# Page numbers of a paged cache: read once into SyncE registers instead of before each page load

## The reference

```
past = lambda pool: pool[layer, page_table].reshape((B, -1) + pool.shape[3:]).astype(z.dtype)
k_all = jnp.concatenate([past(cache_k), k], axis=1)
v_all = jnp.concatenate([past(cache_v), v], axis=1)
```

## Time and profile before

| | us |
|---|---|
| median of 3 runs | 941.52 |
| the three runs | 938.66, 941.52, 942.02 |
| the profiled execution, its own time | 942.91 |
| its span in the trace | 941.0 |
| TensorE busy (matmul) | 859.9 (91%) |
| VectorE, ScalarE, GpSimd busy | 448.6, 334.4, 89.4 |
| mean granted TensorE clock, of full speed | 0.961 |
| moved by DMA | 105.82 MB, mean 112 GB/s |

### The profile page before, as it was taken

One profiled execution on the slowest core, in us unless ns is written; L12 is line 12 of the kernel. 1 busy time (PEld: TensorE's weight loads), 2 busy tenths in 40 slices (PEclk: granted clock), 3 DMA queues, 4 the chain that ended last, 5 costly groups with the idle time before them and its releaser, 6 DMA issues.

```text
span 941.0 us, 11347 instructions
## 1 busy us (share of the span) xinstructions
PE 859.9 (91%) x4136; PEld 645.4 (69%) x4136; DVE 448.6 (48%) x862; ACT 334.4 (36%) x627; POOL 89.4 (10%) x136
## 2 busy tenths in 40 slices
PE   2799999999988986879978999999999999999997
PEld 0377556687735554435767788888888888888875
DVE  0251656999766873231365432234233433344256
ACT  2452543233445562220366342233212341133232
POOL 2141200112523330001010000000000000000000
PEclk9989999998978897999998999999999999999999
DMA  9733311123276566757201222221232222321202
GB/s 312 278 99 100 99 45 45 28 74 101 91 241 224 180 215 202 234 155 235 87 9 56 76 89 90 90 69 65 91 90 75 62 89 90 89 71 64 90 1 100
DMA packets 68778, 105.82 MB, mean 112 GB/s; under 512 B 6987, under 2 KB 32215, under 8 KB 68715
## 3 DMA queue, kind: packets, MB, share of 16 engines
q1 hardware_dynamic: 64194, 96.48, 32.1%
q0 software_dynamic: 3296, 6.39, 2.2%
q10 hardware_dynamic: 1232, 2.23, 0.7%
HBM read 100.04 MB, written 5.15 MB: 112 GB/s over the span
## 4 chain that ended last, share of the span: by engine, by line
PE 75%; DVE 7%; ACT 3%; issue 2%; DMA 2%; SPq 1%; POOL 0%; DVEq 0%; ACTq 0%
PE bank L742 71%; PE bank L745 3%; DMA raw<-in_ada_w 1%; DVE score L1775 1%; DVE small L1771 1%; DVE probs L1851 1%; ACT stage L1261 1%; DVE keys L1656 1%; ACT w_split L1236 1%; SPq L542 1%; SPq L560 0%; DVE x_res L1952 0%; DVE act_lo L1656 0%; DMA pages<-in_cache_k 0%; ACT pv_rows L1261 0%
## 5 line engine op out<-in xcount | busy, mean ns | idle before, releaser
L742 PE MATMUL bank<-act_hi,w_split 128*128 128x512 f32 (+1 forms) x800 | 265.5, 399 | 1.5 <-DVE q_lo L1659 1.5
L742 PEld LDWEIGHTS bank<-act_hi,w_split 128*128 128x128 f32 (+1 forms) x800 | 150.9, 189 | 37.9 <-issue 3.9
L493 DVE TENSOR_TENSOR w_split<-raw,w_split 128x2048 fp32r<-128x2048 f32 (+2 forms) x47 | 105.5, 2247 | 124.6 <-ACT w_split L1236 124.5
L742 PE MATMUL bank<-w_split,hid_hi 128*128 128x512 f32 x512 | 159.2, 392 | 0.0
L742 PE MATMUL bank<-act_lo,w_split 128*128 128x512 f32 (+1 forms) x400 | 157.1, 393 | 0.0
L1236 ACT ACTIVATE w_split<-raw 128x2048 fp32r<-128x2048 f32 (+2 forms) x48 | 89.3, 1863 | 92.3 <-PE bank L742 92.3
L742 PEld LDWEIGHTS bank<-w_split,hid_hi 128*128 128x128 f32 x512 | 95.9, 188 | 20.7
L742 PE MATMUL bank<-w_split,hid_lo 128*128 128x512 f32 x256 | 100.2, 391 | 0.0
L742 PEld LDWEIGHTS bank<-act_lo,w_split 128*128 128x128 f32 (+1 forms) x400 | 75.5, 189 | 14.5
L1261 ACT ACTIVATE stage<-bank 128x512 f32<-128x512 f32 (+3 forms) x51 | 30.1, 590 | 100.3 <-PE bank L742 92.1
L742 PE MATMUL bank<-w_split,act_s 128*128 128x512 f32 (+1 forms) x248 | 60.7, 387 | 1.5 <-DVE out_t L1958 1.5
(11 more groups left out here) (249 smaller groups left out, 1094.8 us busy)
## 6 DMA issues: line engine op xcount, KB each, us to landing
raw<-in_w_ff SPq DMA_DIRECT2D x32, 1024.0 KB, 5.3
raw<-in_ada_w SPq DMA_DIRECT2D x20, 1024.0 KB, 5.6
raw<-in_w_in SPq DMA_DIRECT2D x10, 1024.0 KB, 5.2
pages<-in_cache_k SPq DMA_DIRECT2D x32, 256.0 KB, 3.1
v_pages<-in_cache_v SPq DMA_DIRECT2D x32, 256.0 KB, 3.0
pages<-in_ada_w SPq DMA_DIRECT2D x4, 1024.0 KB, 13.0
raw<-in_w_out SPq DMA_DIRECT2D x4, 1024.0 KB, 6.4
x_in<-in_x_prompt SPq DMA_DIRECT2D x1, 2048.0 KB, 14.8
```

The costliest lines, as they stand in the source:

```text
L493: return ops.tensor_tensor(lo, r, hi.bitcast(F32), ALU.subtract)
L742: return nc.tensor.matmul(out, lhsT, rhs, start=start, stop=stop, skip_group_check=True)
```

## The change

The reads leave `load_pages`. SP waits once for the table, behind the wait of the piece `k` 0, and after each piece from `k` 0 on reads four page numbers into registers of its own, until it has all 32; they are kept to the end of the pages. Key and value page loads take the address from the kept register.

```diff
@@ -536,11 +536,6 @@
-            def page_of(i):
-                if i == 0:
-                    sp.wait_ge(S["table_in"], 16)
-                return sp.value_load(table[0:1, i:i + 1], min_val=0, max_val=ck.shape[0] - 1)
-
@@ -551,14 +546,18 @@
             for n in range(2, AT[("k", 0)]):
                 load_piece(n)
 
+            page = []
+            sp.wait_ge(S["table_in"], 16)
             for n in range(AT[("k", 0)], AT[("ada", 12)] + 2):
                 load_piece(n)
+                for i in range(len(page), min(len(page) + 4, DB * NPG)):
+                    page.append(sp.value_load(table[0:1, i:i + 1], min_val=0, max_val=ck.shape[0] - 1))
 
             def load_pages(b, cache, slots, landed):
 
                 for g in range(NPG):
                     sp.dma_start(slots[:, b % 2, g, :],
-                                 cache[bass.ds(page_of(b * NPG + g), 1)].rearrange("o p n -> (o p) n"))\
+                                 cache[bass.ds(page[b * NPG + g], 1)].rearrange("o p n -> (o p) n"))\
                         .then_inc(landed[b % 2], 16)
```

## The result

| | before | changed |
|---|---|---|
| median of 12 runs each, us | 943.24 | 939.06 |
| the runs | 938.66 to 946.84 | 932.47 to 943.42 |
| profiled execution, us | 942.91 | 936.69 |
| its span, us | 941.0 | 934.8 |
| mean granted TensorE clock | 0.961 | 0.968 |

The account below looks back on a forecast made before the run. TensorE was taken to bound the kernel, waiting in the decode attention for pages SP issued late. Savings of 4.7 + 3.0 + 0.3 + 0.6 = 8.6 us from median 941.5 gave 932.9, stated as 933.2 us; range 930 to 938.

Parts of the forecast that it names:

- the clock falls all the same: Rival: short idle times in the decode attention still halve TensorE's clock, so 5.6 us saved, 935.9 us; chance 0.22.
- Part 1: First decode pair: pages issued without reads cut TensorE's wait for sequence 2's keys from 5.43 to 0.7 us, saving 4.7.
- under 5.5: Sign that the forecast is right: SP issues the twelve pages of the first burst within 5.5 us of about 347.
- The row of 370 GB/s: Rate taken for the first burst from modulation weight loads: eleven pages in 7.8 us, landing at 358.2.
- Part 2: Behind the wait for sequence 2's keys TensorE's clock no longer falls to half: 3.0 us saved.
- Part 3: Last decode pair: its 0.28 us wait for value pages goes, 0.3 us saved; the half clock there stays.
- Part 4: Start of the prompt's attention: earlier first key pages let the next modulation weight load land sooner, 0.6 us saved.
- Part 5: Page number reads moved between the eight weight loads are covered by SP's free time there: cost 0.
- The premise that a gain before 500 us comes through whole: From 500 us on TensorE is busy 431.66 of 435 us, so whatever is gained earlier is kept in full.
- the transfers did not bind at 247 GB/s: Rival: page transfers, not their issue, limit the first burst, so 1.8 us saved, 939.7 us; chance 0.11.
- crowding did not choke the queue: Rival: twelve pages in flight slow each other, under 160 GB/s for a loss over 0.5%, 947.0 us; chance 0.03.
- the change did what it says: Denies the rival that register copies cost as much as the reads, burst 8.8 us, time 941.5; chance 0.04.

Follow-up runs that it names:

- e5: The kernel before, with six matmuls whose result nothing reads put in TensorE's wait for the key pages of sequence 2; ratio 0.9975 to the kernel before.
- e1: The changed kernel with kept page numbers only for the twelve pages of the first burst, other pages reading theirs at the load; 0.9956 of the kernel before.
- e2: The changed kernel, all 32 numbers kept, but the twelve pages of the first burst read theirs again at the load; 0.9997 of the kernel before.
- e3: The kernel before with each page number of the first burst read twice, the first value thrown away; ratio 1.0087 to the kernel before.
- e4: The changed kernel with the keys of sequences 2 and 3 issued before the values of 0 and 1; 0.9925 of the kernel before.
- e8: The changed kernel, but the first eight key pages (sequences 0 and 1) read their numbers at the load; 0.9944 of the kernel before.
- e7: The changed kernel with matmuls that nothing reads in TensorE's waits for the softmax of each pair; 0.9904 of the kernel before.
- e9: The changed kernel with keys of sequences 2 and 3 first, first eight key pages read at load, unread matmuls in the softmax waits; 0.9888 of the kernel before.

## Why the prediction was right, and where not

The saving was forecast as 8.6 us and measured as 5.3, between 3.0 and 7.5, so it was overrated. The direction holds, and on the footing of the three runs 936.2 lies in the range, whose top was 938. The median of 939.06 itself is above it, because the kernel before was 1.7 us slower in the larger sample too. The time alone would speak for the rival that the clock falls all the same, with 5.6 us saved; only the trace of pair 1 and e5 tell that the forecast's mechanism was at work, and that the time came out near that rival for another reason, a fall two pairs later.

- **Part 1, the wait: 4.7 forecast, 4.05 measured.** The last page went out at 352.7 and the transfers took over, as said. The twelve issues took 6.15 us and not under 5.5: a value page without its address arithmetic went out every 0.48 us and not every 0.44, and one issue took 0.78. The row of 370 GB/s was a little too good: the burst moved 350 by its window, and the eleven pages behind the first landed at about 340 (between 350.0 and 358.47), so a wait of 1.4 us stayed instead of 0.7. e1, e2 and e3 show that the twelve reads were the cause; e4 shows that the rest of the wait was the eight value pages ahead in the queue. The 358 GB/s of the Trainium skill ("DMA: Bandwidth & Descriptors", "Where 436 GB/s comes from") gave 4.5, closer than my row; as a ceiling it does not hold here, since the earlier trace rows has 368 and 387.
- **Part 2, the clock: 3.0 forecast, 3.1 measured** in pair 1, confirmed alone by e5. The step that failed is the sentence that the clock would stay up: it did in pair 1, but fell in pair 3 in two (changed, e4) of the four profiled executions with a short wait or none and no fill (changed, e1, e4, e8). The 1.7 us were given back there. It was the rival "the clock falls all the same" in part, at a later place, and no term of mine stood for it. The rule of the Trainium skill that stood with this rival ("TensorE: Matmul & The Clock Gate", "A second HAM failure mode: psum-queue depth-cycling"), short idles that make the clock swing, fits pair 3 of the changed kernel and of e4, and e7, where the fall is gone with the idles; pair 1 does not agree with it, nor does pair 3 of e1 and e8, at full clock with the same idle times.
- **Part 3, the last pair: 0.3 forecast, 0.3 measured** (17.50 to 17.18 us from its logits to the gates), by luck. The 0.28 us of the earlier trace rows were an idle time of the weight loads; the products themselves waited for ScalarE, as they still do. The pair takes 17.17 us in e2 and 17.95 in e8, which both keep the numbers of its value pages and have no such idle time, so its length goes by how long the half clock lasts. That its half clock would stay is right, and e7 shows what it costs.
- **Part 4, the first key pages: 0.6 saved forecast, nothing found.** 0.5 to 1.1 us are lost at the first modulation piece and gone by the fourth, and e8 has the changed kernel's ratio. I read 0.70 us of one execution as a cost that could be won, and looked only at SP's queue. ScalarE waits for a store that lands late beside the faster burst.
- **Part 5, the reads: 0 forecast, 0 found.** The slowest read took 0.490 us, the first four were done 2.9 us behind the weight issue, and the next issue came 7.8 us behind it. e2 has all 32 reads and no loss.
- **The premise that a gain before 500 us comes through whole** held for the changed kernel, whose profiled execution needs the same 509.6 us behind the stage, but not in every execution, as e9 shows.
- **The rivals:** the transfers did not bind at 247 GB/s, and crowding did not choke the queue. The clock rival came true in part. The reads are gone from the burst, so the change did what it says.

With what is shown, 4.05 + 3.1 - 0.85 (1.7 us in half of four profiled executions) = 6.3 us, inside the measured interval. This sum was made after the result, and four executions are few for the share of one half; it shows that the terms are compatible with the time, not more.

## What to carry to other kernels

When the queue of an engine that only issues transfers stands in the chain, count its time per transfer and multiply by the burst behind one release: twelve pages at 1.08 us were a wait of 5.4 us, while the same reads placed where that engine waits anyway cost nothing. Price the wait together with the clock behind it, here 5.4 and 3.1 us, and reckon with a part of the latter coming back at a later sparse place; independent matmuls in the idle times held it here. Look in every stretch where the faster engine now bursts for stores of other engines that land later, and follow such a delay on: here it was gone three pieces of work later. Take a wait of under 1 us from a single trace as a cost only when another execution has it too, and a saving of that size as yours only when it is the wait that went away.

## What had not been expected of the hardware

- The granted clock fell in the third pair in changed and e4 but not in e1 and e8, although the instructions of this stretch and the 1.64 us of idle time before it were the same. TensorE was busy for 2.96 of 3.00 us in 388 to 391 while it fell to 0.84 on average, so the fall came after the sparse stretch, during dense work. Likewise in the last pair: idle for 2.94 us, and half clock only behind it. Why the same idle time counts in one execution and not in the other stays open.
- A short store of 256 KB from ScalarE's queue took 4.9 us to land in the crowd of eight page loads, although the store before it in its queue had landed. With the pages read inline the same store took 2.9 to 3.6 us in all other runs, and 4.5 to 4.9 in the four with kept numbers. Separate queues did not keep it apart.
- In the changed kernel the issue of a value page, which has no address arithmetic of its own, took longer, 381 ns in the median instead of 333, so of the time of the arithmetic only a part was won. It is not the crowd: the value pages of the last pair, at 406.7 to 410.0 us, also have 381, and the key pages in the middle of the crowded burst 333. Single issues of 0.5 to 1.0 us occur in the kernel before too (1016 ns for one value page between 385 and 400 us).
